# Gate-weight splits of the second block's attention, one step later in two engines' order

## What is computed

```python
h  = rms_norm(x, g_mix) * (1 + sc_m) + sh_m
z  = h @ w_in + b_in
qa, ka, va, qi, ki, wi, qb, kb, vb, ga, gb = split_cols(z)
y_a = sparse_indexed_attention(qa, ka, va, qi, ki, wi) @ w_oa   # per row the 128 keys of the highest index score
y_b = chunked_band_attention(qb, kb, vb, rel_bias) @ w_ob
merged = sigmoid(ga) * y_a + sigmoid(gb) * y_b
x  = x + gt_m * (merged @ w_out)
h2 = rms_norm(x, g_ffn) * (1 + sc_f) + sh_f
x  = x + gt_f * ((silu(gate(h2)) * up(h2)) @ w_down)
```

## Time and profile before

| | us |
|---|---|
| median of 3 runs | 3168.64 (3160.5 to 3171.4) |
| the profiled execution | 3169.78 |
| its span | 3168.0 |
| its mean granted TensorE clock | 0.946 of full |
| busy: PE / DVE / ACT / POOL | 2805.0 / 1449.4 / 880.8 / 118.0 |
| first 16 steps and a little, layer 0 | 1664 to 1796 |
| the same, layer 1 | 2501 to 2633 |

### The profile page before, as it was taken

The page is one execution under the profiler, slowest core; times in us unless marked ns, Lnnn a source line. Parts: engine busy times, 40 slices in busy tenths (PEclk is TensorE's granted clock), DMA queues, the critical chain, the costliest instruction groups (busy, mean ns, idle before and its releaser), DMA issues.

```text
span 3168.0 us, 48322 instructions
## 1 busy us (share of the span) xinstructions
PE 2805.0 (89%) x21116; PEld 2053.2 (65%) x21116; DVE 1449.4 (46%) x2739; ACT 880.8 (28%) x1432; POOL 118.0 (4%) x197
## 2 busy tenths in 40 slices
PE   6799999998868777783898899999988988999999
PEld 5577777775653332331776677888876666778887
DVE  5554646556551010014466655433356665553433
ACT  3322131313410000002233453322223335432231
POOL 0010101010000000001000000000000000000000
PEclk9899999999978899996999999999999999999999
DMA  4243535353258999994324322333332332323332
GB/s 133 67 152 121 158 102 162 101 155 143 93 234 331 428 428 427 429 428 165 96 82 98 100 89 78 97 100 97 96 85 77 96 77 90 110 80 100 94 99 80
DMA packets 152265, 489.53 MB, mean 155 GB/s; under 512 B 13168, under 2 KB 40432, under 8 KB 139632
## 3 DMA queue, kind: packets, MB, share of 16 engines
q1 hardware_dynamic: 113824, 365.52, 32.3%
q0 software_dynamic: 25840, 94.12, 9.2%
q10 hardware_dynamic: 12384, 26.74, 2.6%
HBM read 456.44 MB, written 29.90 MB: 154 GB/s over the span
## 4 chain that ended last, share of the span: by engine, by line
PE 69%; DVE 12%; DMA 12%; ACT 5%; issue 1%; SPq 0%; POOL 0%; DVEq 0%; ACTq 0%; POOLq 0%
PE psum L156 66%; DMA wslot<-in_w_up 4%; DMA wslot<-in_w_gate 3%; DMA wslot<-in_w_down 3%; PE psum L159 3%; DVE halfL L165 2%; DVE sc__234 L195 1%; ACT halfH L162 1%; DVE m L192 1%; DVE a20S L180 1%; DVE a21S L180 1%; ACT a1S L162 1%; ACT L162 0%; DVE n_xn L168 0%; DVE n_ht L168 0%
## 5 line engine op out<-in xcount | busy, mean ns | idle before, releaser
L165 DVE TENSOR_TENSOR halfL<-ring,halfH 128x1024 fp32r<-128x1024 f32 x302 | 367.5, 1221 | 718.1 <-ACT halfH L162 717.6
L162 ACT ACTIVATE halfH<-ring 128x1024 fp32r<-128x1024 f32 x302 | 316.6, 1053 | 742.6 <-PE psum L156 740.7
L156 PE MATMUL psum<-hH,halfH 128*128 128x512 f32 x1200 | 487.0, 406 | 9.7 <-DVE halfL L165 9.6
L156 PE MATMUL psum<-hL,halfH 128*128 128x512 f32 x1200 | 474.4, 395 | 0.0
L156 PE MATMUL psum<-hH,halfL 128*128 128x512 f32 x1200 | 474.2, 395 | 0.0
L156 PE MATMUL psum<-wslot,XT 128*64 128x512 f32 x1024 | 259.2, 665 | 76.7 <-DMA wslot<-in_w_gate 42.3
L156 PEld LDWEIGHTS psum<-hH,halfH 128*128 128x128 f32 x1200 | 229.2, 191 | 84.9 <-issue 24.0
L156 PEld LDWEIGHTS psum<-hH,halfL 128*128 128x128 f32 x1200 | 229.1, 191 | 49.7
L156 PEld LDWEIGHTS psum<-hL,halfH 128*128 128x128 f32 x1200 | 229.4, 191 | 44.2
L156 PEld LDWEIGHTS psum<-wslot,XT 128*64 128x64 f32 x1024 | 90.4, 152 | 244.7 <-issue 243.5
L156 PE MATMUL psum<-halfH,hH 128*128 128x512 f32 (+2 forms) x576 | 219.3, 381 | 11.8 <-DVE halfL L165 8.4
(11 more groups left out here) (438 smaller groups left out, 3887.4 us busy)
## 6 DMA issues: line engine op xcount, KB each, us to landing
wslot<-in_w_gate SPq DMA_DIRECT2D x32, 2048.0 KB, 29.8
wslot<-in_w_up SPq DMA_DIRECT2D x32, 2048.0 KB, 29.6
wslot<-in_w_down SPq DMA_DIRECT2D x32, 2048.0 KB, 30.1
ring<-in_w_in SPq DMA_DIRECT2D x120, 512.0 KB, 3.8
ada<-in_w_ada POOLq DMA_DIRECT2D x96, 512.0 KB, 4.2
ring<-in_w_gu SPq DMA_DIRECT2D x88, 512.0 KB, 3.6
ring<-in_w_down SPq DMA_DIRECT2D x44, 512.0 KB, 3.8
gate_rows<-stage ACTq DMA_DIRECT2D x48, 256.0 KB, 2.1
```

The lines of the kernel that those rows point to most:

```text
L156: return self.e.matmul(*a, **k)
L162: return self.e.activation(*a, **k)
L165: return self.e.tensor_tensor(*a, **k)
```

## The change

The splits that belong to step t's gate matmuls are made at step t+1, in the same place of the loop body. On ScalarE the kept results of step t stay at step t, and so come first; on VectorE the split is still ahead of the selection round. TensorE's, GpSimd's and SyncE's programs stay as they are.

```diff
@@ scalar_program, -1653,7 +1653,11
             gates = beside(L)
             for t in attention(A2[L]):
                 for step, *x in gates.get(t, []):
-                    (gate_tile if step == "gates" else gate_kept)(*x)
+                    if step == "kept":
+                        gate_kept(*x)
+                for step, *x in gates.get(t - 1, []):
+                    if step == "gates":
+                        gate_tile(*x)
@@ vector_program, -2457,7 +2461,7
             gates = beside(L)
             for t in attention(A2[L]):
-                for step, _, c, *x in gates.get(t, []):
+                for step, _, c, *x in gates.get(t - 1, []):
                     if step == "gates" and x[1] == 0:
                         split_to(G_gate2[L][c].tiles[x[0]][0] + 2, LAST)
                 if 1 <= t <= 16:
```

## The result

In the set of runs that gave the result the changed kernel took 3180.2 us (median of 10) against 3167.7 for the kernel before: ratio 1.0044, 95% interval 1.0033 to 1.0055. Measured again in a second set it was 3182.3 against 3160.6, 1.0065 (1.0050 to 1.0080). So it is slower by 12 to 22 us. The forecast was 3190, 21 us over before.

The account below looks back on a forecast made before the run. It took the attention to be a three-engine ring holding TensorE about a fifth of the time. Wait terms made +11.4 us a layer, the clock -1.0: +10.4, +20.8 for two layers, forecast 3190 us, range 3172 to 3204.

Parts of the forecast that it names:

- the clock term: Attention stage: slow-clock stretches after long waits, some new at 1 to 1.6 us each, some gone; -1.0 us a layer.
- Third step: Steps 3, 7, 11, 15 get a split, so TensorE waits ahead of scores 4, 8, 12, 16; +16.7 us a layer.
- First steps of four: Steps 4, 8, 12, 16 lose a split: -0.8 us ahead of scores 9 and 13, -3.1 at step 16.
- Step 17: This step now has the split that stood at step 16; +1.6 us a layer, between 0 and 1.9.
- Steps 6 and 14: ScalarE's split no longer waits for same-step gate matmuls, so waits ahead of scores 7 and 15 go; -3.3 us a layer.
- Steps 2 and 10: ScalarE's matmul wait stays, as a same-step kept result now precedes the split; +0.99 us each, +2.0 a layer.
- Steps 5, 9, 13: Waits ahead of scores 6, 10, 14 become about 2.0, 1.5 and 2.5 us; together -1.4 a layer.
- The sum of waits: TensorE's waits for VectorE's maximum in the first 17 attention steps: near 33 us a layer, not 24.
- The faster one: Rival: ScalarE reaches the splits at steps 3, 7, 11, 15 in time for VectorE; 3156 us, chance 0.08.
- No change: Rival: losses at steps 3, 7, 11, 15 half hidden because TensorE comes late at 1.2 GHz; 3172 us, chance 0.12.
- Slower by far: Rival: every wait near 4 us is followed by a slow-clock stretch and none goes; 3202 us, chance 0.10.
- The hidden parts: Later SyncE ring-buffer loads, splits at steps 0 and 1, GpSimd's queue and ScalarE's DMAs: counted at nothing.

Follow-up runs that it names:

- experiment 1: The changed kernel with ScalarE's split (of the step before) put ahead of the kept results again; ratio 0.9960 to the kernel before.
- Experiment 5: The kernel before with VectorE's selection round moved ahead of its half of the split; 3106.2 us, ratio 0.9807 to the kernel before.
- experiment 7: The kernel before with VectorE's selection round ahead of its split, splits one step later, ScalarE's split ahead of kept results; 3107.4 us, ratio 0.9827.
- Experiment 6: The changed kernel, kept results still ahead of the split, with VectorE's selection round ahead of its split; ratio 0.9850 to the kernel before.

## Why the prediction was right, and where it was not

**Direction and size.** 3190 forecast, 3180 and 3182 measured; the stages give +17.7 and +18.3 for the forecast's +20.8, the runs +12.5 and +21.7. The mechanism, a ring in which VectorE's round and fill queue behind a split that queues behind ScalarE, is what the experiments show. That the sum came so near is in part luck: the waits were 5 us a layer too high and the clock term nearly 4 too low, as shown below. Of what the prediction said would be seen, 3.4 to 4.9 us ahead of scores 4, 8, 12 and 16 came true in the first profile at 8 and 16 only, and 9 to 12 us longer a layer in two of four stages (9.5, 8.1, 8.1, 10.2).

**Term by term,** first profile, layer 0. *Third step:* ahead of scores 8 and 16 I had 4.7 and it was 4.54 and 4.58; the working for scores 8, 9.42 from fill 6 to fill 7, measures 9.41 (1714.49 to 1723.90). Ahead of 4 and 12 I had 3.4 and 3.9 and it was 1.02 and 2.21. There TensorE came late by itself, at the lower clock: step 3 took it 8.20 - 1.02 = 7.18 us, where the like step takes 4.81, and step 11 took 6.47. For step 3 I had booked that as a saving of up to 3.0 under the clock; it came as a wait 2.4 shorter than I had it, while TensorE's own time in step 3 fell by 0.3 only, from 7.51. For step 11 I had booked nothing. *First steps of four:* the 0.41 ahead of scores 9 and 13 went, and 3.88 ahead of 17 went to nothing instead of 0.8. *Step 17:* 1.62 ahead of scores 18 for my 1.6. *Steps 6 and 14:* gone, as said. *Steps 2 and 10:* +0.92 and +0.95 for my 0.99. *Steps 5, 9, 13:* 1.74, 1.25, 2.25 for my 2.0, 1.5, 2.5. At step 5 the chain was as I had it: the copy took 0.76 (1699.38 to 1700.14) for my 0.8, and from its start to scores 6 it is 7.88 for 7.9. It was TensorE that came later: from the copy's start to scores 5, at 1700.19, it is 0.81 for my 0.6.

**The sum of waits** was too high: I expected near 33 us a layer, and the four stages show 28.1, 28.1, 26.6 and 28.2. Against 22.7 to 24.0 that is 4.4 more on average, and 1.8 more after scores 17, where I had 1.6 for step 17 and -0.3 for the rest.

**The clock is the term that was mis-sized,** and it has the wrong sign. I took -1.0 us a layer. The stages are 9.0 longer on average and the waits by 6.3 (for my 11.4), so TensorE's own time grew by 2.7. The granted clock fell from 0.94 to 0.90 and 0.92 over the two stages, and it was 0.89 over 1664 to 1796 of after, below the 0.91 that I had set as the limit there. These stretches of after show where (step 8, step 12, step 16):

```profile
1725.00:1731.00 6.00, 5.64 (x16) 4.40 (x17) 5.05 (x19) 3.19 (x10) 2.75 (x4) 0.54 0.97 119
...
1761.00:1768.00 7.00, 6.36 (x17) 4.99 (x18) 5.33 (x19) 2.11 (x6) 0.00 (x0) 0.52 0.00 0
1797.00:1803.00 6.00, 5.35 (x16) 4.18 (x17) 5.79 (x21) 2.48 (x6) 0.00 (x0) 0.56 0.12 44
```

Step 8 took 9.72 us (1725.36 to 1735.08) for 7.44, so 2.3; step 12 took 10.32, so 2.9; step 16 took 6.70 for 4.69, so 2.0. I had 1.0 to 1.6 for each, from the one stretch after scores 10. The failed step is "the 1.56 measured on the step after scores 10 is lower, and I keep it". That stretch was shorter, as a row of before shows:

```profile
1737.42:1744.00 6.58, 6.58 (x22) 4.78 (x23) 0.16 (x2) 3.60 (x9) 0.00 (x0) 0.74 0.11 42
```

A mean clock of 0.74 over 6.58 us, with the two levels 0.50 and 1.00, is some 3.4 us at the lower one; in the three rows of after it is 5.5, 6.7 and 5.3. The Trainium skill ("TensorE: Matmul & The Clock Gate", section "Terms") has half of the slow time. The trace agrees roughly: half would be 1.7, 2.8, 3.4 and 2.6, and 1.56, 2.3, 2.9 and 2.0 were measured. So what I had wrong was the length of the stretch, and the page's estimate with 6.0 us for each was too high by nearly as much as mine was too low. Besides, step 11 was slow behind its 2.58 us in three of the four stages, 1.6 us each, and I had priced no slow stretch there.

The error was hidden by the waits, which were too high by 5.1 where the clock was too low by 3.7: where TensorE is slow it waits less (ahead of scores 12 it waited 3.77 us where step 11 ran at full clock, and 2.2 where it was slow). In layer 1 of after the same step 12 ran at full clock, 7.33 us from 2608.21 to 2615.54 after a wait of 2.19, so the sum can't be had to better than some 3 us a layer.

**What was attributed wrongly.** Most terms were right as differences of waits, and misleading as causes. I wrote +16.7 to the third step's split and +2.0 to the kept results. The experiments divide otherwise (the number of the experiment in brackets):

| from before | stages, us |
|---|---|
| third step's splits later, split first (4) | +5.7 |
| all splits later, split first (1) | -5.5 |
| kept results first, no split later (2) | +29.4 |
| kept results first, all but the third step's splits later (3) | +0.9 |
| both, the change | +17.7, +18.3 |

Moving the splits gains 5.5, or 11 to 12 when the kept results come first; putting the kept results first costs 29.4, or 23 to 24 with the splits moved. The third step's splits cost 5.7 by themselves and 17 beside the rest of the change, not the 33 of my term for two layers, or the 27 left of it after the gain at steps 6 and 14. The term "steps 2 and 10: it stays, +0.99" was the place of the greater error. It counted what is added to before and not what the move would have freed: 3.54 and 1.63 us ahead of scores 3 and 11 (the earlier trace rows has the second), which experiment 1 shows at zero. The kept result also adds its 0.99 ahead of the splits of four more steps of a layer, 5, 7, 13 and 15. Together that is 3.54 + 1.63, the 0.92 + 0.95 more that after has there, and 4 x 0.99: 11.0 a layer, where the stages of after and of experiment 1 differ by 11.6 a layer. The match is in part chance: ahead of scores 4 and 12 after waits 1.40 and 1.25 less than experiment 1, and TensorE's own time is some 2.5 longer.

**The rivals.** The faster one did not happen: ScalarE did not reach the split in time, and VectorE idled 4.07 us. Its mechanism, the half-buffer wait, was real, and with the split ahead of the kept results it does win, by 5.5 us in the stages and 12 in the runs. But it wins otherwise than I had it: the waits ahead of scores 4, 8, 12 and 16 stay, and those ahead of 3 and 11 go. "No change" rested on TensorE coming late in the slow stretches, and it did, ahead of scores 4 and 12. It was no free cover: the slow time was paid as TensorE's own. The rule beside it, that gains come from the most-contended engine (the Trainium skill, "Perfetto Trace Analysis", section "Identifying Performance Opportunities"), names TensorE. Experiment 5 changed nothing on TensorE, only the order on an engine busy for 46% of the span, and saved 61 us: the gain came out of TensorE's waits. That is no case against the page, whose section goes on to look for the gaps on that engine and to make what it waits for start sooner; my "the time would stay at 3169" took its first sentence alone. "Slower by far" has the clock right in part: each wait of 4.4 us or more ahead of scores in the first profile of after was followed by a slow stretch, and behind scores 8 and 16 of layer 0 it cost 2.3 and 2.0, more than the 1.6 I gave. Experiment 5, without such waits, has no slow stretch.

The hidden parts stayed hidden: no DMA appears among the waits of the stage, and between and behind the stages nothing moved by over 0.6 us.

## What to carry to other kernels

In a ring of engines with fixed orders, ask of each instruction that waits for another engine what stands behind it that doesn't need the wait. Putting the 2.97 us of independent selection ahead of the waiting split was worth three to five times what the whole shift of splits was (61 us against 12 to 22), in the other direction. When an edit both moves a wait away and moves another instruction in front, cost the two apart, each against the kernel without the other, since only then does it show that one of them is a gain. And a wait ahead of TensorE has two prices, the wait and the slow stretch behind it, which trade against each other; take the price of a slow stretch from several of them, and look at how long each lasted.

## What the runs showed of the hardware

With no wait ahead of any scores over 2.0 us, the granted clock was 1.00 over the whole of both stages in experiments 5 and 7, against 0.94 in before: of the 27.5 us that experiment 5 saved in layer 0, TensorE's busy time is 8.6 (137.51 to 128.88). Experiment 6, with no longer waits, had 1.00 in layer 0 and a slow stretch in layer 1, behind a wait of 1.98 us ahead of scores 18:

```profile
2581.00:2588.50 7.50, 7.48 (x50) 5.30 (x50) 1.39 (x7) 3.74 (x11) 0.47 (x1) 0.77 0.20 70
```

The step took 7.49 us there; behind the same 1.98 us in layer 0, and in both layers of experiment 7, it took 5.91.

Over the twelve profiles, all 60 waits of 3.2 us or more ahead of scores 2 to 24 were followed by a step that was at least 1.4 us longer than the same step at full clock. Waits from 1.6 to 2.9 us go either way: 2.21 us ahead of scores 12 was followed by the lower clock in layer 0 of after, and 2.19 in layer 1 was not; 1.64 us ahead of scores 15 was followed by it in layer 1 of before (6.40 us for 4.83) and not in layer 0.

Before the attention, with the same code, scores 1 of layer 0 stood anywhere from 1653.1 to 1665.4 us in twelve profiles.

A kept result costs ScalarE 1.0 us in series although its copy takes 0.6: in the rows of step 10 the issue of its DMA (0.33 us) stands between, and the next instruction starts 0.40 us after the copy's end.
